# A tuned two-block transformer kernel: first weight units split in quarters, and one split moved behind the differential output in the second mixer

## What is computed

```python
def first_block(x, ...):
    for l in range(2):
        x = x + 0.5 * swiglu(rms_norm(x, g1[l]), w_gate[l], w_up[l], w_down[l])   # hidden 2816
        x = x + hybrid_mixer(rms_norm(x, gm[l]), w_in[l], ...)
        x = x + 0.5 * swiglu(rms_norm(x, g2[l]), ...)
    return rms_norm(x, g_final)

def second_block(x, ...):
    for l in range(2):
        proj = rms_norm(x, attn_norm[l]) @ w_in[l]
        ya = sparse_attention(aq, ak, av, iq, ik, iw, k_sel)       # 8 heads
        yb = rms_norm(diff_attention(bq, bk, bv, lam), b_subln)    # 4 heads, "differential"
        x = x + (g_a * (ya @ w_up_a) + g_b * (yb @ w_up_b)) @ w_out[l]
        x = x + (silu(h @ w_gate) * (h @ w_up)) @ w_ffn_out[l]     # h = rms_norm(x, ffn_norm)
```

## Time and profile before

| | us |
|---|---|
| median of 3 runs | 1788.2 (1788.02 to 1789.97) |
| the profiled execution, its own time | 1788.07 |
| its span, first to last instruction | 1786.4 |
| PE busy | 1773.3 |
| DVE busy | 1231.7 |
| ACT busy | 988.0 |
| DMA, over the span | 316.26 MB, 177 GB/s |

### The profile page before, as it was taken

The page is one execution under the profiler, slowest core; times in us unless marked ns, Lnnn a source line. Parts: engine busy times, 40 slices in busy tenths (PEclk is TensorE's granted clock), DMA queues, the critical chain, the costliest instruction groups (busy, mean ns, idle before and its releaser), DMA issues.

```text
span 1786.4 us, 25450 instructions
## 1 busy us (share of the span) xinstructions
PE 1773.3 (99%) x9448; PEld 1479.0 (83%) x9448; DVE 1231.7 (69%) x1753; ACT 988.0 (55%) x1333; POOL 226.2 (13%) x255
## 2 busy tenths in 40 slices
PE   9999999999999999999999999999999999999999
PEld 8888877888888888877888877778888877788887
DVE  6775667677557755767776489976775599867763
ACT  6554586565445554666555476555554466645551
POOL 0000131000000000320000096200001383100000
PEclk9999999999999999999999999999999999999999
DMA  8756472555546564544665563535656544545651
GB/s 266 221 195 203 138 211 73 188 188 188 212 145 195 194 224 143 190 119 143 195 197 198 166 212 124 181 128 182 201 195 207 168 162 143 188 159 173 192 202 75
DMA packets 221517, 316.26 MB, mean 177 GB/s; under 512 B 14168, under 2 KB 162288, under 8 KB 221168
## 3 DMA queue, kind: packets, MB, share of 16 engines
q1 hardware_dynamic: 221392, 315.02, 54.1%
q10 hardware_dynamic: 32, 0.01, 0.0%
HBM read 313.94 MB, written 1.05 MB: 176 GB/s over the span
## 4 chain that ended last, share of the span: by engine, by line
PE 84%; DVE 9%; DVEq 3%; ACT 2%; issue 1%; ACTq 0%; POOL 0%; POOLq 0%
PE ps L2091 25%; PE ps L1955 14%; PE ps L1957 13%; PE ps L1956 13%; PE ps L2092 13%; DVE w_lo L1222 3%; PE ps L1965 1%; ACT w_hi L717 1%; PE ps L2206 1%; PE ps L2179 1%; DVEq L1706 1%; PE ps L2194 1%; DVEq L1742 1%; DVE score L1731 1%; DVE att L1755 1%
## 5 line engine op out<-in xcount | busy, mean ns | idle before, releaser
L1222 DVE TENSOR_TENSOR w_lo<-raw,w_hi 128x2048 fp32r<-128x2048 f32 (+2 forms) x296 | 674.5, 2301 | 200.9 <-ACT w_hi L717 199.2
L2091 PE MATMUL ps<-aT,w_hi 128*128 128x512 f32 x1920 | 667.9, 392 | 0.0
L717 ACT ACTIVATE w_hi<-raw 128x2048 fp32r<-128x2048 f32 (+2 forms) x296 | 551.5, 1891 | 158.9 <-PE ps L1957 155.7
L2092 PE MATMUL ps<-aT,w_lo 128*128 128x256 f32 x1920 | 537.7, 280 | 0.0
L2091 PEld LDWEIGHTS ps<-aT,w_hi 128*128 128x128 f32 x1920 | 359.2, 187 | 79.8 <-issue 0.3
L2092 PEld LDWEIGHTS ps<-aT,w_lo 128*128 128x128 f32 x1920 | 362.9, 189 | 0.2
L1955 PE MATMUL ps<-w_hi,aT 128*128 128x512 f32 (+2 forms) x768 | 309.3, 403 | 4.3 <-DVE w_lo L1222 2.8
L1957 PE MATMUL ps<-w_hi,aT 128*128 128x512 f32 (+2 forms) x768 | 295.1, 384 | 0.0
L1956 PE MATMUL ps<-w_lo,aT 128*128 128x512 f32 (+2 forms) x768 | 294.2, 383 | 0.0
L1955 PE MATMUL ps<-w_hi,gT_hi 128*128 128x512 f32 x528 | 206.0, 390 | 0.0
L1957 PE MATMUL ps<-w_hi,gT_lo 128*128 128x512 f32 x528 | 205.6, 389 | 0.0
(11 more groups left out here) (289 smaller groups left out, 1704.0 us busy)
## 6 DMA issues: line engine op xcount, KB each, us to landing
raw<-in_w_in SPq DMA_DIRECT2D x120, 512.0 KB, 4.6
raw<-in_w_ffn_down SPq DMA_DIRECT2D x88, 512.0 KB, 4.4
raw<-in_w_ffn_in SPq DMA_DIRECT2D x88, 512.0 KB, 5.0
raw<-in_w_ffn_gate SPq DMA_DIRECT2D x86, 512.0 KB, 4.1
raw<-in_w_ffn_up SPq DMA_DIRECT2D x86, 512.0 KB, 5.1
raw<-in_w_ffn_out SPq DMA_DIRECT2D x44, 512.0 KB, 4.7
raw<-in_w_out SPq DMA_DIRECT2D x32, 512.0 KB, 4.7
raw<-in_w_ck SPq DMA_DIRECT2D x8, 512.0 KB, 3.9
```

The source lines that it names most:

```text
L717: nc.scalar.activation(dst, src, ACT.Copy).then_inc(units_hi, 1)
L1222: V.tensor_tensor(o, a, h, ALU.subtract).then_inc(units_split, 1)
L2091: M(o, wh, aT[:, :, k, :], start=k == 0, stop=False, skip_group_check=True)
L2092: r = M(o[:, 0], wl, aT_hi[:, k, :], start=False, stop=k == KC - 1, skip_group_check=True)
```

## The change

Two places are touched, in both cases by order and grain alone; the arithmetic stays the same.

At the start, units 0 and 1 are split in quarters of 512 columns, one for each column block, and PE waits for each quarter. The four transposes of part 0 of x go to two banks (4 and 2), and DVE begins the low part when ACT has done the first two of its four pieces. ACT and DVE take all of unit 0 ahead of part 1 of x, and parts 1 and 2 ahead of unit 1. Unit 2 is split in two halves. 24 filling transposes become 22.

In the second mixer (both layers), ACT runs `diff_hi` ahead of the split of unit `P2_UP + 1`, and DVE runs `diff_lo` and `gate(10, 0)` ahead of it.

```diff
@@ scalar engine @@
+            def first_stage():
+                act.wait_ge(stage_T, 1)
+                for c in range(4):
+                    o = nc.scalar.activation(aT_hi[:, c, 0:P], ps[:, FIRST_BANKS[c // 2], P * c:P * c + P], ACT.Copy,
+                                             scale=gain_cols[:, GAIN_FFN1 + c:GAIN_FFN1 + c + 1])
+                    if c % 2 == 1:
+                        o.then_inc(stage_hi if c == 3 else first_hi, 1)
+            def first_quarters(j, h):
+                act.wait_ge(loaded[j] if h else half_loaded[j], 32)
+                for c in (2 * h, 2 * h + 1):
+                    part = slice(512 * c, 512 * c + 512)
+                    nc.scalar.activation(w_hi[:, j, part], raw[:, j, part], ACT.Copy)\
+                        .then_inc(units_hi if c == 3 else quarter_hi, 1)
...
-                    stage(0, GAIN_FFN1, FIRST_PARTS[:1])
-                    first_half(0, 0)
-                    first_half(0, 1)
+                    first_stage()
+                    first_quarters(0, 0)
+                    first_quarters(0, 1)
                     stage(0, GAIN_FFN1, FIRST_PARTS[1:2], first=1)
-                    first_half(1, 0)
                     stage(0, GAIN_FFN1, FIRST_PARTS[2:3], first=2)
-                    first_half(1, 1)
-                    stage(0, GAIN_FFN1, FIRST_PARTS[3:], first=3)
-                    split(st, 2)
+                    first_quarters(1, 0)
+                    first_quarters(1, 1)
+                    stage(0, GAIN_FFN1, FIRST_PARTS[3:4], first=3)
+                    third_unit()
...
                 exps(7)
+                diff_hi()
                 split(st, P2_UP + 1)
-                diff_hi()
                 split(st, P2_UP + 2)
@@ vector engine @@
+            def first_quarters(j, h):
+                for c in (2 * h, 2 * h + 1):
+                    if c == 3:
+                        dve.wait_ge(units_hi, j + 1)
+                    else:
+                        dve.wait_ge(quarter_hi, 3 * j + c + 1)
...
                 probs(7)
-                split(st, P2_UP + 1)
                 diff_lo()
                 gate(10, 0)
+                split(st, P2_UP + 1)
                 split(st, P2_UP + 2)
                 probs_turned(7)
@@ tensor engine @@
-                        if i == 0 and c == 0:
-                            pe.wait_ge(half_split, j + 1)
-                        if i == 0 and c == 2:
+                        if i == 0 and c < 3:
+                            pe.wait_ge(quarter_split, 3 * j + c + 1)
+                        if i == 0 and c == 3:
                             split_ready(st, j)
...
-            first_turned(0)
-            busy(24)
+            pe.wait_ge(x_loaded[0], 16)
+            for c in range(4):
+                o = nc.tensor.transpose(ps[:, FIRST_BANKS[c // 2], P * c:P * c + P], x[:, 0, P * c:P * c + P], ident[:, :])
+            o.then_inc(stage_T, 1)
+            busy(22)
```

More of the change, by code:

```diff
@@ L245, in build @@
         gains_T = sem("gains_T")
+        first_hi = sem("first_hi")
+        quarter_hi = sem("quarter_hi")
+        quarter_split = sem("quarter_split")
         half_hi = sem("half_hi")
[L247 removed]
         gains_ready = sem("gains_ready")
@@ L817, in rope, with third_unit @@
                                          ACT.Sin).then_inc(rope_sin, 1)
-            def first_half(j, h):
-                act.wait_ge(loaded[j] if h else half_loaded[j], 32)
-                part = slice(1024 * h, 1024 * h + 1024)
-                nc.scalar.activation(w_hi[:, j, part], raw[:, j, part], ACT.Copy).then_inc(units_hi if h else half_hi, 1)
+            def first_stage():
[6 more added lines that the diff above has]
+            def first_quarters(j, h):
+                act.wait_ge(loaded[j] if h else half_loaded[j], 32)
+                for c in (2 * h, 2 * h + 1):
+                    part = slice(512 * c, 512 * c + 512)
+                    nc.scalar.activation(w_hi[:, j, part], raw[:, j, part], ACT.Copy)\
+                        .then_inc(units_hi if c == 3 else quarter_hi, 1)
+            def third_unit():
+                act.wait_ge(loaded[2], 32)
+                nc.scalar.activation(w_hi[:, 2, 0:1024], raw[:, 2, 0:1024], ACT.Copy).then_inc(half_hi, 1)
+                nc.scalar.activation(w_hi[:, 2, 1024:2048], raw[:, 2, 1024:2048], ACT.Copy).then_inc(units_hi, 1)
             act.dma_start(first_rows[:, :], I["norm_ffn1"].rearrange("l (c p) -> (l c) p", p=P))\
@@ L1403, in other_gains, with first_stage, third_unit @@
                 rope()
[L1405 to L1410, removed]
+            def first_stage():
+                for c in range(4):
+                    if c == 0:
+                        dve.wait_ge(first_hi, 1)
+                    if c == 2:
+                        dve.wait_ge(stage_hi, 1)
+                    o = V.scalar_tensor_tensor(aT_lo[:, c, 0:P], ps[:, FIRST_BANKS[c // 2], P * c:P * c + P],
+                                               gain_cols[:, GAIN_FFN1 + c:GAIN_FFN1 + c + 1],
+                                               aT_hi[:, c, 0:P].bitcast(F32), ALU.mult, ALU.subtract)
+                o.then_inc(stage_ready, 1)
+            def first_quarters(j, h):
[4 more added lines that the diff above has]
+                        dve.wait_ge(quarter_hi, 3 * j + c + 1)
+                    part = slice(512 * c, 512 * c + 512)
+                    V.tensor_tensor(w_lo[:, j, part], raw[:, j, part], w_hi[:, j, part].bitcast(F32), ALU.subtract)\
+                        .then_inc(units_split if c == 3 else quarter_split, 1)
+            def third_unit():
+                dve.wait_ge(half_hi, 1)
+                V.tensor_tensor(w_lo[:, 2, 0:1024], raw[:, 2, 0:1024], w_hi[:, 2, 0:1024].bitcast(F32), ALU.subtract)
+                dve.wait_ge(units_hi, 3)
+                V.tensor_tensor(w_lo[:, 2, 1024:2048], raw[:, 2, 1024:2048], w_hi[:, 2, 1024:2048].bitcast(F32),
+                                ALU.subtract).then_inc(units_split, 1)
             dve.wait_ge(gains_T, 1)
@@ L1419, in _ @@
                 if l == 0:
-                    stage(0, GAIN_FFN1, FIRST_PARTS[:1])
-                    first_half(0, 0)
-                    first_half(0, 1)
+                    first_stage()
+                    first_quarters(0, 0)
+                    first_quarters(0, 1)
                     stage(0, GAIN_FFN1, FIRST_PARTS[1:2], first=1)
-                    first_half(1, 0)
+                    stage(0, GAIN_FFN1, FIRST_PARTS[2:3], first=2)
+                    first_quarters(1, 0)
+                    first_quarters(1, 1)
                     dve.wait_ge(x_loaded[0], 16)
@@ L1427, in _ @@
                     dve.sem_inc(x_ready, 1)
-                    stage(0, GAIN_FFN1, FIRST_PARTS[2:3], first=2)
-                    first_half(1, 1)
+                    stage(0, GAIN_FFN1, FIRST_PARTS[3:4], first=3)
                     dve.wait_ge(x_loaded[1], 16)
```

1 line of the change is left out of this document (added).

## The result

The changed kernel takes **1793.85 us** (median of 11 executions, 1791.03 to 1795.18), the kernel before 1788.2 (11 executions beside them, 1787.85 to 1790.41). The ratio is 1.0022 with a 95% interval of 1.0014 to 1.0030: slower by 5.6 us, where 0.5 was forecast and the range ended at 1790.2. The profiled execution took 1794.14 us, its span is 1792.4.

What follows compares the result with a forecast made beforehand. PE was taken as the bound, busy 1773.3 us of a span of 1786.4. The sum was 1788.07 - 0.85 (start) + 0.88 + 0.62 (second mixer, two layers) = 1788.72, so 1788.7 us, range 1786.8 to 1790.2.

Steps and rivals of the forecast that it cites:

- The mixer's arithmetic: Second mixer: the `yb_lo` wait goes, but DVE's late copy delays `sparse_pv(7)` by 0.88 us in layer 0, 0.62 in layer 1.
- the sum of the prediction: Second mixer, layer 0: gate 0.84, two splits of 2.21, copy 0.55 and wake-up 0.14 us before `sparse_pv(7)`.
- Rivals 1 and 3: Rival 1: mixer's first wait goes, nothing follows, 1785.0, chance 0.08; rival 3: mixer neutral, start gains 0.85, 1787.2, chance 0.12.
- Rival 2: Start gives nothing and the second mixer has its loss: 1789.6 us, chance 0.12.
- rival 4: Idle before `sparse_pv(7)` lets PE's clock fall, both layers pay 3.0 us: 1791.7, chance 0.04; sign: matmuls 0.4 us apart.
- The argument against it: Against the clock falling in the mixer: idle of 0.84 and 0.88 us did not lower it, matmuls behind stay 0.23 us apart.
- The start term: Start: first product 1.0 us earlier, part 1 of x turned 0.80 earlier, 0.85 us gained; bounds 0.55 and 1.1.
- the fast step: Start: the 24 filling transposes from 4.71 us take 0.13 us each, read as PE at 2.4 GHz.
- the lower bound: Start: gain of only 0.55 us if part 1 of x lands 0.3 us later.
- the upper bound of the prediction: Start: gain of 1.1 us if part 1 of x lands in time and the transfer sets nothing.
- the start's gain is kept up to the second block: Behind 21.29 us PE has no listed wait until the second block, so the start's 0.85 us is kept.
- The range: Whole kernel: 1786.8 to 1790.2 us, taking in the forecast and rivals 2 and 3, leaving out rivals 1 and 4.

Runs made afterwards that it cites:

- e5_five_drains: The kernel before with five drains, which do nothing, at the head of DVE's program, start and mixer unchanged: 1789.47 us, ratio 1.0008.
- e1_start_only: The changed start alone, against the kernel before, with `diff_hi` and `diff_lo` where they were: 1789.13 us, ratio 1.0004.
- e3_mixer_filled: The kernel before with the changed mixer order alone, plus 14 unused transposes on PE ahead of `sparse_pv(7)`: 1789.69 us, ratio 1.0006.
- e7_after_late_pv: The changed kernel with `sparse_pv(7)` moved three column blocks later into the next phase: 1787.17 us, ratio 0.9995 to the kernel before.
- e9_start_fill12: The changed start alone, with five DVE instructions fewer and 12 filling transposes instead of 22: 1787.35 us, ratio 0.9993 to the kernel before.

## Why the prediction was wrong, step by step

In the profiled execution the forecast's 1788.72 became 1794.14. The difference is made of 3.1 us for two falls of the clock, which the sum put at nothing; 0.7 for a start that gave 0.17 instead of 0.85; 1.4 for a moved pause of DVE, and 0.3 for one of ACT, which no term had.

**The mixer's arithmetic was right.** The wait for `yb_lo` went, the gate waited for the half-tile signal (0.57 us, 0.6 forecast), and the copy came late by the sum of the prediction: net 0.91 and 0.55 us against 0.88 and 0.62, and 1.89 us of idle against 1.9. The run with the mixer alone and a filled stretch gives 1.3 us for the two by medians. The two runs that free the product from the copy confirm which step decides, the one that moves the product by its median, the one that moves the copy in its profile and in four of ten executions. Rivals 1 and 3 fall. Rival 2 is right that the start gives next to nothing in the changed kernel, and wrong that this is all.

**The step that failed most is the weight given to rival 4.** It was named, with its sign in the trace (matmuls 0.4 us apart) and its price (1.5 us a layer; measured 1.55), and given 0.04. The argument against it was that 0.84 us and 0.88 us of idle had not lowered the clock; but these are half the length that the prediction itself worked out. No row stood for the length in question, so they could not carry 24 to 1. By the mean granted clock it fell in eight of the eleven executions of the mixer alone, and twice in seven of the changed kernel's eleven. It is not certain in any one of them: three executions of the mixer alone and one of the changed kernel (1791.03) had no fall.

**The start term was mis-sized: 0.85 forecast, 0.1 to 0.2 in the changed kernel's profile.** The quarters did what was worked out in four of seven profiles (DVE done at 7.42 to 7.53, first product possible at 7.6). Three things stood in the way. The first is a step that the prediction took over without asking: that PE's fillers end near 7.8 as they did before, or sooner with 22. They end when the clock lets them, 7.5 us in one execution and 8.8 in the next: the 24 of the kernel before took 3.05 us in its profile, and 4.04 in that of `e5_five_drains`, which has the same start. The mean of 0.13 us each, which the prediction calls the fast step, already mixed the two: the steps are 0.21 us and then 0.11. One profile can't show that spread, and the prediction named no condition for the fillers at all. The second is the transfer of x, which set the turning at 8.94 in one execution, 0.37 later than forecast; the lower bound had 0.3. The third is the landing of unit 0: in three of seven profiles ACT waits for it until 6.40 to 6.59 us (6.04 forecast), and DVE's first quarter is done at 7.76 to 7.95. The kernel before has this spread as well: its old start has the first product at 8.60 in three profiles, and at 8.63, 8.84 and 9.17 in the others. With the fillers cut and DVE's pauses back in their old places, the start is worth 1.1 us by medians (1788.43 against 1787.35), the upper bound of the prediction, but the interval takes in no change, and the profile has 0.7.

**A term was missing altogether: 1.2 to 1.4 us for five more instructions on DVE.** The prediction counted their fixed parts and found them hidden, which they are. That they move a pause in all that follows was in no step. Its sentence that the start's gain is kept up to the second block fails the same way, at the 0.29 us near 250 us that come with ACT's moved pause. The pauses could be seen beforehand, as "issue" rows of DVE with nothing to wait for. The Trainium skill, page "Runtime: NRT & Kernel Launch", section "Instruction fetch mechanics", has each engine refill its instruction memory in blocks, and calls the cost of crossing one mostly hidden. If these pauses are that, the trace shows 0.24 to 0.49 us, and hidden or not is decided by the instruction on which it falls.

**The range** left out rival 4 and had no room for the missing term. By medians: before 1788.2, start and shifted program +0.8, mixer with its falls +3.0, together 1792.0; the changed kernel is at 1793.85. Its executions with both falls are more frequent than those of the mixer alone (seven of eleven against two). Why is open.

## What to carry to other kernels

When an edit removes a wait, follow the engine that served it to the end of its queue: whatever stood behind still does, and the wait may come back there, longer and in one piece. Move the last item of that chain too, or the consumer (2.4 us faster here, from 3.0 slower). And where the new idle stretch is longer than any in the trace, the cheap state of the clock is not a fact but a guess: price it, and give it an honest chance, or fill the stretch. Last, an edit that adds instructions moves the pauses of that engine in all that follows: look where they fall before a loss far from the edit is put down to its data flow.

## What the runs showed of the hardware that was not expected

An idle stretch of 1.9 us on a tensor engine that was busy on both sides was enough to halve its clock in most executions, at 1.55 us each time. Stretches of 0.9 and 1.2 us (1132.78 in the changed kernel) did not in any profile. Length alone doesn't decide: of four profiles with a stretch of 2.3 us near 1032 us, three show the clock at 0.50, 0.54 and 0.56 behind it (`e1_start_only`, `e3_mixer_filled`, `e7_after_late_pv`) and one at 1.00 (`e5_five_drains`), and 1.70 us at the start of `e9_start_fill12` did nothing.

What is read here as instruction fetch shows as a pause at fixed numbers of DVE's program, 0.45 to 0.49 us at the one that counted. GpSimd, whose program the change leaves alone, has its own pauses of 0.24 and 0.43 us on the same two instructions in both kernels.

The kernel before has two groups of times, near 1788.1 and near 1790.0, and the others have them too. The profiles of both kinds differ at one place, where a long run of small GpSimd instructions meets a split of DVE. The kernel before, DVE and then GpSimd:

```profile
1027.40 2.48 DVE L1222 TENSOR_TENSOR w_lo<-raw,w_hi 128x2048 fp32r<-128x2048 f32 x1 [0.68 <-ACT w_hi L717]
...
1024.03 7.72 POOL L674 TENSOR_TENSOR rg<-cs,par 128x64 f32<-128x64 f32 x20 [236.43 <-DVE xn L1284]
```

And `e5_five_drains`, with PE behind them:

```profile
1027.61 4.44 DVE L1222 TENSOR_TENSOR w_lo<-raw,w_hi 128x2048 fp32r<-128x2048 f32 x1 [0.68 <-ACT w_hi L717]
...
1024.24 5.67 POOL L674 TENSOR_TENSOR rg<-cs,par 128x64 f32<-128x64 f32 x20 [236.43 <-DVE xn L1284]
...
1032.11 0.50 PE L1957 MATMUL ps<-w_hi,aT 128*128 128x512 f32 x1 [2.29 <-DVE w_lo L1222]
```

Either DVE takes 2.48 us and GpSimd 7.72, or DVE takes 4.44 and GpSimd 5.67: one of them waits out 2 us for the other, and where it is DVE, PE waits 2.29 us behind it. That is 1.83 us in the offset, about the distance of the groups. The Trainium skill, page "SBUF — State Buffer", section "Who interferes with whom", says that an instruction of DVE with two inputs from SBUF contends with one of GpSimd that reads SBUF, and calls the contention an exclusive lock; the rows agree. The profiles of `e1_start_only`, `e3_mixer_filled`, `e5_five_drains` and `e7_after_late_pv` are of the longer kind, the other nine of the shorter, and the four profiled executions stand 1.7 to 2.2 us over their medians. That the same kernel goes now one way and now the other is read from its two groups of times; no kernel was profiled both ways.
